# Attention stage: results of 64 rows written in pairs to opposite halves of TensorE, their matmuls alternating

## What is computed

```python
def compress(t, w1, w2, pos_emb):                     # of keys and of values, 2 groups, 15 blocks of 32 tokens
    ch = t.reshape(B, n_chunk, NSA_CMP_STRIDE, G, dh)
    blk = jnp.concatenate([ch[:, r:r + n_cmp] for r in range(ratio)], axis=2)
    blk = (blk + pos_emb[:, None, :]).transpose(0, 1, 3, 2, 4).reshape(B, n_cmp, G, NSA_CMP_LEN * dh)
    return jax.nn.gelu(blk @ w1) @ w2
kc = compress(k_cmp, cmp_w1[0], cmp_w2[0], cmp_pos[0])
vc = compress(v_cmp, cmp_w1[1], cmp_w2[1], cmp_pos[1])
s_c = jnp.einsum('bqgjd,bcgd->bgjqc', qb, kc) * scale - slopes * dist_c      # compressed scores
o_c = jnp.einsum('bgjqc,bcgd->bqgjd', masked_softmax(s_c, dist_c >= 0), vc)
...                                                   # every kind of head ends in such a product
o_s = jnp.einsum('bgjqk,bgqkd->bqgjd', p_s, vs)       # probabilities x values -> 64 features a head
return g[..., 0:1] * o_c + g[..., 1:2] * o_s + g[..., 2:3] * o_w
```

## Time and profile before

| | us |
|---|---|
| median of 3 runs | 2823.4 |
| lowest, highest | 2819.6, 2832.94 |
| profiled execution, span of the core | 2821.3 |
| the attention stage within it, PE's first to last projection matmul (L3008) | 1519.8 to 1926 |
| next stage's first matmul | 1938.0 |

### The profile page before, as it was taken

The page is one execution under the profiler, slowest core; times in us unless marked ns, Lnnn a source line. Parts: engine busy times, 40 slices in busy tenths (PEclk is TensorE's granted clock), DMA queues, the critical chain, the costliest instruction groups (busy, mean ns, idle before and its releaser), DMA issues. The chain is left out here.

```text
span 2821.3 us, 51247 instructions
## 1 busy us (share of the span) xinstructions
PE 2697.4 (96%) x19853; PEld 2445.7 (87%) x19853; DVE 1960.6 (69%) x2805; ACT 1411.4 (50%) x2327; POOL 325.2 (12%) x496
## 2 busy tenths in 40 slices
PE   7899999989899999999998999998999999999998
PEld 4689898878788888999998888887878888889998
DVE  2388986788777777887876588785588755555554
ACT  3355657654445555445444454555344444444454
POOL 1001412121011110111110112220011000000000
PEclk9999999999999999999999999999999999999999
DMA  9967666538388887987883766664578665665553
GB/s 362 338 236 239 205 236 195 195 92 296 122 295 275 288 278 248 306 282 264 279 264 87 214 218 216 229 215 136 164 247 292 229 186 179 189 187 185 178 189 132
DMA packets 290941, 632.51 MB, mean 224 GB/s; under 512 B 31490, under 2 KB 52422, under 8 KB 290502
## 3 DMA queue, kind: packets, MB, share of 16 engines
q1 hardware_dynamic: 239120, 484.78, 51.9%
q0 software_dynamic: 40192, 142.63, 15.0%
q10 hardware_dynamic: 11446, 2.54, 0.6%
HBM read 627.77 MB, written 2.10 MB: 223 GB/s over the span
## 5 line engine op out<-in xcount | busy, mean ns | idle before, releaser
L1218 DVE TENSOR_TENSOR weight_parts<-weights,weight_parts 128x1024 fp32r<-128x1024 f32 x584 | 707.1, 1222 | 300.2 <-ACT weight_parts L1138 298.9
L1138 ACT ACTIVATE weight_parts<-weights 128x1024 fp32r<-128x1024 f32 x584 | 607.0, 1057 | 560.9 <-PE accumulators L1329 251.4
L1318 PE MATMUL accumulators<-h_parts,weight_parts 128*128 128x512 f32 x2816 | 776.5, 397 | 18.9 <-DVE h_parts L1205 8.5
L1318 PEld LDWEIGHTS accumulators<-h_parts,weight_parts 128*128 128x128 f32 x2816 | 485.2, 190 | 88.3 <-DVE h_parts L871 9.4
L1329 PEld LDWEIGHTS accumulators<-h_parts,weight_parts 128*128 128x128 f32 x2944 | 451.7, 190 | 69.5 <-DVE weight_parts L1218 8.5
L1329 PE MATMUL accumulators<-h_parts,weight_parts 128*128 128x256 f32 x2944 | 472.2, 282 | 6.2 <-DVE weight_parts L1218 6.1
L1364 PE MATMUL accumulators<-h_parts,weight_parts 128*128 128x256 f32 x1728 | 433.3, 283 | 0.0
L1366 PE MATMUL accumulators<-h_parts,weight_parts 128*128 128x256 f32 x1728 | 433.3, 283 | 0.0
L1366 PEld LDWEIGHTS accumulators<-h_parts,weight_parts 128*128 128x128 f32 x1728 | 331.8, 192 | 0.0
L1364 PEld LDWEIGHTS accumulators<-h_parts,weight_parts 128*128 128x128 f32 x1728 | 331.7, 192 | 0.0
L1804 PE MATMUL accumulators<-in_h_parts,in_weight_parts 128*128 128x256 f32 x1024 | 263.6, 289 | 20.6 <-DVE in_weight_parts L2112 20.2
(11 more groups left out here) (411 smaller groups left out, 3104.2 us busy)
## 6 DMA issues: line engine op xcount, KB each, us to landing
weights<-in_w_ff SPq DMA_DIRECT2D x256, 512.0 KB, 5.4
weights<-in_w_in SPq DMA_DIRECT2D x160, 512.0 KB, 5.4
wide<-in_w_ada SPq DMA_DIRECT2D x112, 512.0 KB, 10.6
h_t<-in_ada_w POOLq DMA_DIRECT2D x96, 512.0 KB, 6.7
weights<-in_ffn_w_gate SPq DMA_DIRECT2D x88, 512.0 KB, 4.5
weights<-in_ffn_w_up SPq DMA_DIRECT2D x88, 512.0 KB, 4.5
weights<-in_ffn_w_down SPq DMA_DIRECT2D x88, 512.0 KB, 4.0
weights<-in_w_out SPq DMA_DIRECT2D x64, 512.0 KB, 4.9
```

The costliest lines, as they stand in the source:

```text
L1138: nc.scalar.activation(w[:, held:held + take, 0, :], core.ring[:, q % RING, k:k + take, :], ACT.Copy).then_inc(core.high_ready, take)
L1218: ins = nc.vector.tensor_tensor(w[:, held:held + take, 1, :], core.ring[:, q % RING, k:k + take, :], w[:, held:held + take, 0, :].bitcast( ...
L1318: nc.tensor.matmul(core.ps[:, nt, :], high, x[:, kt].rearrange("p a t -> p (a t)"), start=(kt == 0), stop=False, skip_group_check=True)
```

## The change

- Compressions: the 32 matmuls for keys and the 32 for values alternate; keys accumulate in rows 0 to 63, values in rows 64 to 127 of the bank. Bursts are six matmuls each, the last four. ACT reads the two halves with two instructions.
- Compressed scores: both banks are claimed first, and the matmuls of group 0 (input rows 0 to 63) and of group 1 (64 to 127) alternate. The count is the same.
- Heads of 64: the first of a pair is written to rows 0 to 63, the second to 64 to 127 of the bank, both with 64 weight columns, and their matmuls alternate. No padding is left. ACT copies from those rows to the head's place in `hT`. Single heads take rows 0 to 63. Pairs of 128-row heads (diff) stay in sequence.
- `mix.VC` loses its 64 padding columns, and POOL the memset of them.

```diff
+    def head_rows(y, width):
+        return slice(0, P) if width == P else slice(HD * y, HD * y + HD)
...
-                for a in range(2):
-                    at = 2 * a * N_CMP
-                    for l in range(32):
-                        ins = nc.tensor.matmul(ps[0:HD, bank, at:at + 2 * N_CMP], mix.W1[:, a, l, :], blk[:, a, l, :],
-                                               start=(l == 0), stop=(l == 31))
-                        if l % 6 == 5:
-                            yield
+                for l in range(32):
+                    for a in range(2):
+                        at = 2 * a * N_CMP
+                        ins = nc.tensor.matmul(ps[HD * a:HD * (a + 1), bank, at:at + 2 * N_CMP], mix.W1[:, a, l, :],
+                                               blk[:, a, l, :], start=(l == 0), stop=(l == 31), skip_group_check=True)
+                    if l % 3 == 2:
+                        yield
...
-                for g in range(GROUPS):
-                    rows = slice(g * HD, (g + 1) * HD)
-                    bank = for_scores.claim(pe, ("cmp_scores", g), "dve")
-                    for n in range(4 * TT):
+                cmp_banks = [for_scores.claim(pe, ("cmp_scores", g), "dve") for g in range(GROUPS)]
+                for n in range(4 * TT):
+                    for g, bank in enumerate(cmp_banks):
+                        rows = slice(g * HD, (g + 1) * HD)
...
-                        up = width == HD and row % P == HD
...
-                                    parts.append((k * P, SEQ, tok[:, k, col - HD * up:col + width], PT[:, n % 2, a:b]))
-                        height = HD + HD * up if width == HD else P
-                        for z, (a, b, lhsT, rhs) in enumerate(parts):
-                            ins = nc.tensor.matmul(ps[0:height, bank, y * SEQ + a:y * SEQ + b], lhsT, rhs,
-                                                   start=(z == 0), stop=(z == len(parts) - 1),
-                                                   skip_group_check=True)
+                                    parts.append((to, k * P, SEQ, tok[:, k, col:col + width], PT[:, n % 2, a:b]))
+                        sums.append(parts)
+                    terms = range(len(sums[0]))
+                    if pair[0][1] == P:
+                        order = [(y, z) for y in range(len(sums)) for z in terms]
+                    else:
+                        order = [(y, z) for z in terms for y in range(len(sums))]
+                    for y, z in order:
+                        to, a, b, lhsT, rhs = sums[y][z]
+                        at = y * SEQ
+                        ins = nc.tensor.matmul(ps[to, bank, at + a:at + b], lhsT, rhs, start=(z == 0),
+                                               stop=(z == len(sums[y]) - 1), skip_group_check=True)
...
-                nc.scalar.activation(hid[:], ps[0:HD, bank, 0:4 * N_CMP], ACT.Gelu_apprx_tanh
-                                     ).then_inc(for_scores.releases("act", "hidden"), 1)
+                for n in range(2):
+                    at = slice(2 * n * N_CMP, 2 * (n + 1) * N_CMP)
+                    ins = nc.scalar.activation(hid[:, at], ps[HD * n:HD * (n + 1), bank, at], ACT.Gelu_apprx_tanh)
...
-            nc.gpsimd.memset(mix.VC[:], 0.0).then_inc(s["masks_ready"], 1)
+            nc.gpsimd.memset(blk, 0.0).then_inc(s["masks_ready"], 1)
```

## The result

| | before | with the change |
|---|---|---|
| median us (lowest to highest), same call | 2822.02 (2818.53 to 2832.94), 6 runs | 2805.4 (2803.03 to 2809.33), 6 runs |
| ratio, 95% interval | | 0.9937 [0.9923, 0.9951] |
| the same two kernels in a later call | 2823.24 (2817.35 to 2827.52), 12 runs | 2809.31 (2803.62 to 2814.57), 6 runs |
| ratio, 95% interval | | 0.9952 [0.9938, 0.9967] |
| profiled execution, span | 2821.3 | 2802.2 |

The change saves some 15 us. The second set puts it a little lower than the first; the twelve runs of the changed kernel together have a median of 2807.8. The forecast was 2807.9, in the right place and, as the rest shows, partly for wrong reasons: two terms of the sum were off by about 5 us each, in opposite directions.

What follows compares the result with a forecast made beforehand. PE was taken as the bound. Its work falls by 3.4 + 2.0 + 8.1 + 4.0 - 0.5 = 17.0 us, less 1.5 lost to DVE: net 15.5, forecast 2807.9 us, range 2800 to 2819.

Steps and rivals of the forecast that it cites:

- The price of a pair: Alternating matmuls of 64 weight columns to opposite result halves: a pair costs what one did, 32 records in 1.08 us.
- Compressions: Bursts of 12 records, run as six pairs, fall from 0.82 to 0.50 us; 3.4 us saved in all.
- nsa heads: Four packs: a pair takes one head's 2.01 us instead of 4.03 or 4.15; 8.1 us saved.
- the six pairs: Three fox and three dil pairs take 0.80 us instead of 1.47 each; 4.0 us saved.
- entry and exit of a burst: In the compression bursts, some 0.2 us that might not shrink, making 0.52 us the upper bound.
- Compressed scores: Their 32 records, 4.06 us before, run as 16 paired steps; 2.0 us saved.
- Claiming both banks ahead adds no wait: At the compressed scores: the compressions' bank was released in slot 54, twelve slots before, so no time is lost.
- DVE's give-back: PE waits after shorter bursts: 0.4 us behind nsa pack 1, 0.6 behind pack 3, 0.4 after 1882; 1.5 in all.
- rival 1: DVE takes over behind nsa packs 1 and 3 and after 1782: 5.5 us more lost, 2813.4 us; chance 0.22.
- rival 3: Half clock near the compressed scores goes with their shorter burst: 3 us more gained, 2804.9 us; chance 0.22.
- rival 2: Streams of 256 columns take turns, so nsa, fox and dil heads gain nothing: 5 us gained, 2818 us; chance 0.10.
- rival 4: Each record of the alternating bursts waits for its weights: 13 to 18 us added, 2836 us; chance 0.03.

Runs made afterwards that it cites:

- e5: The changed kernel with both heads of a pair written to rows 0 to 63, matmuls still alternating; 2821.0 us (one run).
- e6: The kernel before with only 4 of the 16 modulation products of a chunk and their loads; 2814.3 us, ratio 0.9972.
- e2: The kernel before with the compressed scores alone alternating between the input halves; ratio 0.9988.
- f3: The changed kernel with the compressed scores in sequence, one half after the other; 2809.5 us, ratio 0.9955.
- f4: The changed kernel with a chunk's modulation products spread over 18 slots instead of 13, their sum in slot 20 instead of 14; 2802.0 us, ratio 0.9932.
- e7: The changed kernel with only 4 of the 16 modulation products of a chunk and their loads; 2789.9 us, ratio 0.9881.
- second pair of executions: The kernel before and the changed one run once more, nothing edited; 2827.1 us (one run) and 2809.3 us.
- e4: The changed kernel with a pair's two heads still in opposite halves but in sequence, not alternating; 2815.9 us, ratio 0.9973.

## Why the prediction was right where it was, and wrong where it was

- **The price of a pair** (rows 5): right, and it carried the forecast. Compressions 3.6 us saved for 3.4, nsa heads 8.2 for 8.1, the six pairs 4.2 for 4.0, singles 0.4 lost for 0.5. e5 shows that the opposite halves are the cause. One small reading was wrong: the 0.2 us for entry and exit of a burst doesn't follow from 16 records in 1.08 us and 12 in 0.82, as a straight line through these leaves 0.04. The 0.47 us measured lies between the prediction's 0.41 and 0.52.
- **Compressed scores**, 2.0 us: mis-sized. At full clock the burst took 3.28 (e6), so the pairs save 1.4; the row of 4.06 that I halved lay in part at half clock, as rows 10 of the same forecast say. The other 0.8 of its 2.17 is clock.
- **"Claiming both banks ahead adds no wait"**: wrong. I looked at the claim of those two banks, not at the next claim of the ring. PE reaches that one sooner and finds DVE's release late: 1.3 us (1.7 in e2, none in f3 and f4).
- **DVE's give-back, 1.5 us**: the step that failed, by 4.8 us with the bank's. Measured it is 6.3, 0.3 of it ACT's and about 5.3 gone in e7; it may be more in the second pair of executions. PE's waits for DVE grew by 3.9 us in the first pair (2.6 for low parts, 1.3 for the bank) and by 6.6 in the second. I had located the losses behind packs 1 and 3 and at the end. Behind pack 1 nothing was lost; behind pack 3 it was 1.2, not 0.6; and 1.0 by the compressed scores, 1.4 right behind them, 1.3 behind the third fox pair and 1.2 after that were not in the sum, as I had judged DVE by its idle time before the first low part behind a burst. A low part is late where modulation product, sum and scores stand in a row, and those clumps lie some slots on. In kind this is rival 1 (5.5 us beyond the forecast's), with the loads of the modulation as its second half: DVE's waits for them went from 8.9 to 10.0.
- **The clock, rival 3** (chance 0.22): happened. I priced the stretch of rows 10 at 3 us on top; by the table it is 2.2 behind the burst and 0.8 inside. Another 1.7 at 1820 is in the difference of these two executions only.
- **Sharing of streams (rival 2)** is excluded, with 2.03 us for a pair of 256 columns. **Slower (rival 4)** too: forty-eight records of six pairs now take 4.80 us where they took 8.96. The rule of the Trainium skill ("TensorE: Matmul & The Clock Gate", Part 3, The mechanism), by which a weight load overlaps running matmuls only where its row group differs, does not hold here: both halves use all 128 rows, and 20 records take 2.03 us. The prediction had left aside that the same section also lets a load go ahead when it targets the background weight buffer, so its rival followed from one sentence of the page and not from the whole.

So 17.0 of work was right; 1.5 given back should have been 6.3, and a clock gain of about 5, of which 3 lasts, should have been in the likeliest case. The two offset each other: that the number came out was luck in its last steps, and is no proof of them.

## What to carry to other kernels

Two f32 matmuls with 64 weight columns and all input rows cost what one does here (2.03 us for an nsa pair, 2.01 for one head) when they go to opposite row halves of the result and stand next to each other in PE's stream; padding to 128 columns throws that away. When PE gets shorter bursts, don't judge the engine that feeds it by its idle time behind those bursts: look for the places where several pieces of its side work stand in a row, and spread them (f4, 6 us). And when banks of a ring are claimed earlier, check the next claim of the same ring too.

## What the runs showed of the hardware that I had not expected

- Records of opposite halves start 7 ns apart when they alternate and 13 ns apart when the program has them four records apart (e4), with the same 0.80 us for the burst. Ten apart, with 15-row records between, they don't overlap at all (4.03 us).
- The granted clock fell to 0.50 within the burst of 32 matmuls of 15 columns in five of six executions where it took 3.3 to 4.1 us, and in none of eight where it took 1.9. PE did not stand within the burst in either case.
- Two matmuls to the same half with different columns don't overlap when they alternate: 3.75 us for an nsa pair against 4.03 in sequence (e5, e4). The 0.28 between them is about what the second change to records of 15 rows and back costs in e4 (0.20 before 1689.80 and 0.30 before 1690.38, where records in a row follow at 0.11 or 0.22); that is only argued.
- With both heads' sums in the same rows of a bank, in different columns and begun alternately, e5's values come out wrong; in opposite rows of the same bank they are right.
